# Context keys and values in one stage, and norm factors taken up by the last projection

## What is computed

```python
hc = rms_norm(h_ctx, norm_g[l]) * (1.0 + scale_c) + shift_c
...
kv = hc @ w_in[l][:, ATT_W:ATT_W + 2 * KV_W]
kc_raw, vc_raw = kv[..., :KV_W], kv[..., KV_W:]
```

```python
yb = rmsnorm(o_b.reshape(B, S, HG_WIDTH), hg_norm_w[l]) * jax.nn.silu(hg_g)
...
yc = (yc + ssd_d[l][:, None] * xs_h).reshape(B, S, SSD_WIDTH) * jax.nn.silu(ssd_z)
yc = rmsnorm(yc.reshape(B, S, SSD_GROUPS, SSD_WIDTH // SSD_GROUPS), ...)
y = jnp.concatenate([ya, yb, yc], axis=-1) @ w_out[l]
x = x + gate[:, None] * y
return rmsnorm(x, final_norm_w)
```

## Time and profile before

| | us |
|---|---|
| median of 3 runs (4582.68 to 4587.5) | 4583.03 |
| the profiled execution | 4579.17 |
| its span | 4577.5 |
| TensorE busy | 3936.8 (86%) |
| VectorE busy | 2498.4 (55%) |
| ScalarE busy | 1578.3 (34%) |
| GpSimd busy | 1141.5 (25%) |

### The profile page before, as it was taken

One profiled execution on the slowest core, in us unless ns is written; L12 is line 12 of the kernel. 1 busy time (PEld: TensorE's weight loads), 2 busy tenths in 40 slices (PEclk: granted clock), 3 DMA queues, 4 the chain that ended last, 5 costly groups with the idle time before them and its releaser, 6 DMA issues. The chain is left out here.

```text
span 4577.5 us, 51311 instructions
## 1 busy us (share of the span) xinstructions
PE 3936.8 (86%) x19136; PEld 3218.8 (70%) x19136; DVE 2498.4 (55%) x3386; ACT 1578.3 (34%) x2597; POOL 1141.5 (25%) x972
## 2 busy tenths in 40 slices
PE   4659998798795999879879699999997967776998
PEld 1548886687574888668748588878886656665886
DVE  2635943687374594368736653330000479995564
ACT  2332102676221210267622222241111755554331
POOL 0421110121111111012111111111110048885454
PEclk8879999899897999989989899999998979998999
DMA  5342122422473212242246511231121365554553
GB/s 215 123 140 74 74 79 79 105 58 71 152 244 130 73 74 79 79 105 59 65 153 215 183 69 70 82 143 69 69 78 64 129 152 148 148 138 154 183 191 113
DMA packets 315680, 529.46 MB, mean 116 GB/s; under 512 B 26806, under 2 KB 203574, under 8 KB 299512
## 3 DMA queue, kind: packets, MB, share of 16 engines
q1 hardware_dynamic: 276874, 353.84, 24.9%
q0 software_dynamic: 38592, 172.82, 10.1%
HBM read 373.57 MB, written 153.00 MB: 115 GB/s over the span
## 5 line engine op out<-in xcount | busy, mean ns | idle before, releaser
L455 PE MATMUL in_ps<-h,in_wp 128*128 128x512 f32 x6624 | 1508.2, 390 | 9.9 <-POOL in_wp L620 9.9
L455 PEld LDWEIGHTS in_ps<-h,in_wp 128*128 128x128 f32 x6624 | 1246.8, 188 | 271.2 <-POOL in_wp L620 11.6
L1696 PE MATMUL out_ps<-out_y,out_wp 128*128 128x512 f32 x2976 | 691.7, 394 | 32.1 <-ACT out_y L1551 26.9
L1696 PEld LDWEIGHTS out_ps<-out_y,out_wp 128*128 128x128 f32 x2976 | 564.2, 190 | 159.3 <-issue 32.3
L590 DVE SCALAR_TENSOR_TENSOR cy<-cu,in_cw,cy 128x2048 f32<-128x2048 f32 x120 | 314.5, 2621 | 4.3
L880 PE MATMUL att_O<-att_pT,att_vs 128*128 128x512 f32 x960 | 302.6, 424 | 0.0
L518 ACT ACTIVATE in_ob<-in_ps 128x2048 f32<-128x2048 f32 x37 | 69.7, 1885 | 664.1 <-PE in_ps L455 664.1
L1613 POOL TENSOR_TENSOR out_wp<-out_w,out_wp 128x2048 fp32r<-128x2048 f32 (+1 forms) x48 | 192.6, 4011 | 412.7 <-ACT out_wp L1544 412.6
L620 POOL TENSOR_TENSOR in_wp<-in_w,in_wp 128x1024 fp32r<-128x1024 f32 x75 | 201.7, 2691 | 291.0 <-ACT in_wp L468 255.1
L1004 DVE TENSOR_TENSOR att_pT<-att_T,att_pT 128x512 fp32r<-128x512 f32 x320 | 219.5, 686 | 74.1 <-ACT att_pT L933 65.8
L1959 DVE TENSOR_SCALAR hi_z<-hi_z 128x4 f32<-128x4 f32 x1 | 0.2, 169 | 463.2 <-ACT hi_z L1916 463.2
(11 more groups left out here) (483 smaller groups left out, 6262.7 us busy)
## 6 DMA issues: line engine op xcount, KB each, us to landing
in_w<-in_w_in SPq DMA_DIRECT2D x75, 512.0 KB, 3.5
gates<-in_ob POOLq DMA_DIRECT2D x36, 1024.0 KB, 4.2
out_w<-in_w_out SPq DMA_DIRECT2D x32, 1024.0 KB, 4.9
out_mw<-in_w_ada_rows SPq DMA_DIRECT2D x48, 512.0 KB, 3.8
att_qf<-q SPq DMA_DIRECT2D x64, 256.0 KB, 4.3
out_yr<-y SPq DMA_DIRECT2D x16, 1024.0 KB, 7.0
x<-out_x POOLq DMA_DIRECT2D x64, 256.0 KB, 3.9
out_yr<-y SPq DMA_DIRECT2D x32, 512.0 KB, 5.6
```

The source lines that it names most:

```text
L455: mm = nc.tensor.matmul(ps[:, q, c * W:(c + 1) * W], wp[:, q, i, k], h[:, j, k, c * W:(c + 1) * W], start=(n + k == 0), stop=(n == 2 and k ...
L1696: mm = nc.tensor.matmul(ps[:, u % NB, :W], wp[:, u % NW, a, k], y[:, c % 2, b, k], start=(i + k == 0), stop=(i == 2 and k == KY - 1))
```

## The change

It has two parts that don't touch each other.

The first replaces the two stages of the second layer's context by one, `context_keys` (names `ckc_`). SP loads the norm row, half of x, the weights of the keys, the other half of x, the weights of the values. ScalarE copies the weights' heads in one instruction each and between them the heads of h, GpSimd makes the weights' rests, and TensorE makes the values right behind the keys.

```diff
-            sp.dma_start(wt[:], w).then_inc(w_in, 16)
...
+            sp.dma_start(rb[:], row_d.broadcast_to([P, N])).then_inc(row_in, 16)
+            for i, w in enumerate((wk_d, wv_d)):
+                half = slice(i * KH, (i + 1) * KH)
+                sp.dma_start(x[:, half], x_d[half].rearrange("k p t -> p k t")).then_inc(x_in[i], 16)
+                sp.dma_start(wt[:, i], w).then_inc(w_in[i], 16)
...
+        @block.scalar
+        def _(act):
+            for i in range(2):
+                act.wait_ge(w_in[i], 16)
+                nc.scalar.activation(wp[:, i, 0], wt[:, i], ACT.Copy).then_inc(led, 1)
+                for k in range(i * KH, (i + 1) * KH):
+                    act.wait_ge(scaled, k + 1)
+                    nc.scalar.activation(h[:, 0, k], x[:, k], ACT.Identity, bias=shift[:, k:k + 1]).then_inc(headed, 1)
```

```diff
-            def hscale(c):
-                dve.wait_ge(hrooted, c + 1)
-                tt(ho[:, c % 2], ho[:, c % 2], bcast(hrs[:], H), mul).then_inc(hscaled, 1)
...
-            def norm(u):
-                dve.wait_ge(rooted, u + 1)
-                tt(o[:, u % 4], o[:, u % 4], bcast(rs[:], GT), mul).then_inc(normed, 1)
...
             def store(u):
                 c, g = u // 2, u % 2
-                pool.wait_ge(normed, u + 1)
+                pool.wait_ge(gated, u + 1)
...
+            def factors(u):
+                sp.wait_ge(rooted, u + 1)
+                sp.dma_start(norm_d[1 + u % 2:2 + u % 2, at(u // 2)], rs[0:1, u % 4]).then_inc(rs_out[u % 4], 16)
```

In the last projection:

```diff
             def piece(c, p):
                 m = c * G + p
+                if scaled(c, p) is not None and (p - PLAIN) % 2 == 0:
+                    r = (p - PLAIN) // 2
+                    wait(sp, yscaled, scaled(c, p))
+                    sp.dma_start(rn[:], norms[r:r + 1, cols(c)].broadcast_to([P, W])).then_inc(rn_in, 16)
                 wait(sp, yparted, m - 1)
                 sp.dma_start(yr[:, m % 2], y_d[p * KP:(p + 1) * KP, :, cols(c)].rearrange("k p t -> p k t")).then_inc(y_in[m % 2], 16)
...
-                act.wait_ge(y_in[m % 2], 16 * (m // 2 + 1))
+                if scaled(c, p) is None:
+                    act.wait_ge(y_in[m % 2], 16 * (m // 2 + 1))
+                else:
+                    act.wait_ge(yscaled, scaled(c, p) + 1)
...
-                for a in ahead(u):
-                    piece(*a)
+                catch_up = norms is not None and c and n == SQUARE_AT
+                if not catch_up:
+                    for a in ahead(u):
+                        piece(*a)
...
+            def take(c, p):
+
+                if scaled(c, p) is None:
                     return
+                m = c * G + p
+                dve.wait_ge(y_in[m % 2], 16 * (m // 2 + 1))
+                dve.wait_ge(rn_in, 16 * (c * GROUPS + (p - PLAIN) // 2 + 1))
                 for i in range(KP):
                     k = p * KP + i
-                    ins = stt(y[:, c % 2, 1, k], yr[:, m % 2, i], y_gain[:, k:k + 1], y[:, c % 2, 0, k].bitcast(F32), ALU.mult, ALU.subtract)
-                ins.then_inc(yparted, 1)
+                    ins = stt(yr[:, m % 2, i], yr[:, m % 2, i], y_gain[:, k:k + 1], rn[:], ALU.mult, ALU.mult)
+                ins.then_inc(yscaled, 1)
...
             for p in range(G):
-                piece(0, p)
+                take(0, p)
+                if norms is None:
+                    piece(0, p)
+                elif p:
+                    piece(0, p - 1)
```

More of the change, by code:

```diff
@@ L1483, in fresh, with scaled @@
             return u < U and (not kept or u < KT)
+        PLAIN = 2
+        GROUPS = (G - PLAIN) // 2
+        def scaled(c, p):
+            return c * (G - PLAIN) + p - PLAIN if norms is not None and p >= PLAIN else None
         def ahead(u):
@@ L1604, in _ @@
                         square(v)
+                if catch_up:
+                    for a in ahead(u):
+                        piece(*a)
             root(NCH - 1)
@@ L1796, in _ @@
                 for a in ahead(u):
-                    piece(*a)
+                    take(*a)
+                    if norms is None:
+                        piece(*a)
                 add(u)
+                if norms is not None:
+                    for a in ahead(u):
+                        piece(*a)
                 gather(u)
@@ L2180, in _ @@
                     hload(c + 2)
+                if unit(T - 4) is not None:
+                    factors(unit(T - 4))
+                if late(T - 2) is not None:
+                    hfactors(late(T - 2))
+            for T in range(TICKS, TICKS + 5):
+                if unit(T - 4) is not None:
+                    factors(unit(T - 4))
+                if late(T - 2) is not None:
+                    hfactors(late(T - 2))
+            for r in range(4):
+                sp.wait_ge(rs_out[r], 16 * (U // 4))
+            for r in range(2):
+                sp.wait_ge(hrs_out[r], 16 * (C // 2))
         @block.gpsimd
@@ L2569, in _ @@
                 hg(3)
-                if unit(T - 2) is not None:
-                    norm(unit(T - 2))
-                if late(T) is not None:
-                    hscale(late(T))
         @block.tensor
```

173 lines of the change are left out of this document (94 added, 79 removed).

## The result

The changed kernel takes 4590.8 us (median of 20 runs, 4583.2 to 4601.0), the kernel before, beside it, 4583.0 (20 runs, 4576.1 to 4587.5): a ratio of 1.0017, 95% interval 1.0011 to 1.0024. That is 7.9 us more, where 25 less were forecast; the range, 4541 to 4576, misses it by 15. The profiled execution took 4583.6 us (span 4582.0), 4.5 more than the one of before.

A forecast was written before the change was run, and what follows sets the result against it. VectorE was taken to bound the recurrences and TensorE the last projection. Terms -36 (recurrences), -9 (context), +17 and +3 (last projection) sum to -25: 4554 us profiled, 4558 by the median, range 4541 to 4576.

The forecast's parts named there:

- The recurrences, -36: Recurrences: 48 norm multiplications gone from VectorE save 34 us, the stage's end 2; together -36, from -20 to -41.
- the end of the stage: End of the recurrences: GpSimd's 1.90 us wait for the last norm before the last store goes; 2 us taken, bounds 0 and 3.
- rival 2: Recurrences: GpSimd or the chain product, pick, output becomes the bound; gain 12 in place of 36, time 4582; chance 0.12.
- rival 3: Last projection: scaled piece delays the weights' copy in every unit of three blocks; 45 in place of 3, 4600; chance 0.07.
- whether that time vanishes with the operation or falls on the next one: Recurrences: VectorE's standing still for GpSimd in the removed norms, left open between 27.6 and 38.2 us; 34 taken.
- Context keys and values, -9: Second layer's context stages joined: -7 with values at half clock, -11 if the clock rises early; -9, from -4 to -12.
- The start of the last projection, +17: Last projection's first pieces of y: one load in flight, period 6.6 us in place of 4.1; +17, from +11 to +22.
- The 2 us put down for the clock: Start of the last projection: TensorE, underworked between pieces, stands at half clock when it goes on; 2 us more.
- The rest of the last projection, +3: Last projection, blocks 1 and 2: weights' copy behind a scaled piece, about 2 us of waiting each; +3, from 0 to +10.
- the 1 us given back: Rest of the last projection: the norm row in PSUM takes a block's last scalings out of GpSimd's way, about 1 us back.
- The sign: Whole kernel: faster than before 0.83, within 0.1, slower 0.07.
- rival 1: Start of the last projection: the pieces are not the bound, the start costs 4, time 4545; chance 0.13.

The follow-up runs named there:

- e10: Kernel before with the joined context stage and, in the recurrences, output behind turn and exponents without VectorE's wait; norms stay on VectorE: 29.4 us under the kernel before.
- e9: Changed kernel with all that e5, e6 and e7 changed: 4534.1 us against 4579.1 for the kernel before.
- e5: Changed kernel without VectorE's wait for the output, output moved behind turn and exponents, VectorE's products of x ahead of its gates: 19.9 us under the kernel before.
- e4: Changed kernel whose first VectorE difference of a chunk no longer waits for the output of the chunk before: 11.2 us over the kernel before.
- e2: Kernel before with the norms' part alone (factors stored by the recurrences, multiplied in the last projection), old context stages: 23.7 us over the kernel before.
- e3: Changed kernel, VectorE splitting each piece of y right behind its scaling at the last projection's start: 6.4 us over the kernel before.
- e6: Changed kernel with e3's order, and the row of factors asked for behind the first load of y of its pair: 1.8 us under the kernel before.
- e8: Changed kernel as it is, timed again and profiled a second time: 9.9 us over the kernel before, recurrences 494.8 us.
- e7: Changed kernel, ScalarE copying the last projection's weights ahead of its copy of y's next piece: 2.8 us over the kernel before.
- e1: Kernel before with the joined context stage alone: 9.8 us under the kernel before.
- e11: Changed kernel with e5's order on TensorE and VectorE, but VectorE's wait for the output kept: 10.1 us under the kernel before.

## Why the prediction was wrong

**The recurrences, -36: the failed step.** The prediction prices the 46 norms that "lie where VectorE has no gaps" at VectorE's own time, 27.6 to 38.2 us. VectorE had no gaps, but 99% busy did not make its work the thing that sets the pace. The term measured -13.8 in the first profile, -5.4 in the second, and -20 with the path mended (e10 to e9 and e5). In the first profile its small part, the end of the stage, came to -3.1 for -2, so the 34 measured 10. Two things are wrong in it. First, the ring through the output was named (rival 2, "the chain product, pick, output"), given 0.12, and set aside because GpSimd and TensorE "are seen waiting for VectorE", with a fifth to spare. A ring needs no busy engine: it is made of a stretch on each, and each waits for the one before it. Rival 2's 12 us is near what the first profile shows. Its 4582 is the nearest of the times named, 9 us under the measured one; rival 3's 4600 is as near by luck, since no wait for weights in every unit was there. (The Trainium skill, "Perfetto Trace Analysis", Identifying the Most-Contended Engine, says to work first on the engine with the highest occupancy, and takes occupancy on VectorE for a fair measure. The prediction reasoned the same way, and e4, e5 and e10 show where it misleads: VectorE at 99% gave 17 us of stage to a change of order alone.) Second, "whether that time vanishes with the operation or falls on the next one": it fell on other ones (0.9 us a chunk, e5 against e10), while the value taken, 34, lay nearer the bound at which it vanishes.

**The clock in the recurrences: not in the prediction at all.** TensorE stood 2.38 us ahead of the output in the kernel before too, and kept the upper level there. With the norms gone and the output early, five of seven profiles (e2, e3, e4, e6, e8) had 5 or 6 of the 16 outputs at the lower level, 8 to 10 us in all; e7 and the first profile had none. In those five every low output but the very first of e8 stands behind 2.38 us without a product. Such stops from the fifth or sixth chunk on come before every second output, where in e7 and the first profile they come before every fourth. But the kernel before had them before every second output, too, from the sixth on, and kept the upper level, so why some executions have it and others don't stays open. e1 had it in 2 of 16 with the norms in place.

**Context keys and values, -9: right.** The stage fell by 11.2 and the kernel by 9.8 (e1). The values' products began at 1447.8 (1447.3 worked out; the prediction's own steps add up to 1447.0). They took 5.87 us. The clock rose within the first third of them, as reckoned: it was at the lower level up to about 1448.6, which makes 0.84 of full on average from 1448 to 1450, and at the upper one behind that:

```profile
1447.79 5.87 PE L720 MATMUL ckc_ps<-ckc_wp,ckc_h 128*128 128x128 f32 x48
...
1448.00:1450.00 2.00, 2.00 (x17) 2.00 (x17) 0.00 (x0) 0.38 (x1) 0.00 (x0) 0.84 0.23 70
```

That is not so in every execution. In e1, e10 and e11 the same products, behind the same keys, stayed at the lower level to their end, and the stage took 32.5 to 32.9 us, 7 less than before. In e1:

```profile
1445.80 10.34 PE L720 MATMUL ckc_ps<-ckc_wp,ckc_h 128*128 128x128 f32 x48
```

The prediction had both values, -7 and -11, and took -9 between them, so this term was right by its mechanism and rests on the clock for 4 us. The other profiles with the joined stage show 27.5 to 29.1. Why the clock rises in some isn't known.

**The start of the last projection, +17: right.** Period 6.57 (6.6), first full unit 16.3 later: 0.9 up to the third piece's scaling, 12.4 for the five pieces, 2.9 from there to the unit, where 0.6, 12.6 and 1.4 were worked out. The 2 us put down for the clock can't be seen as such. It did fall between the pieces (0.74 of full from 4193 to 4214), but the first full unit ran at the upper level, 16 products in 3.90 us. The cause, one load in flight in place of two, is shown by e3 and e6 in the period, and only in part in the unit's start: with the order mended the period is 5.28, and with the queue behind the factors mended too, 4.44. The second of these, a load standing behind the row of factors, the prediction had not seen, since the first hid it.

**The rest of the last projection, +3: mis-sized.** The mechanism, a copy of y ahead of the weights' copy at the start of blocks 1 and 2, was right and in the right place, but it cost 3.75 + 3.05 us in place of 2 + 2, and the 1 us given back did not show. Of the stage's +26.6, 16.3 is the start, 0.9 the wait behind the first unit's first products, 6.8 these waits; 2.6 is not placed.

**The sign.** Put together: -11 for the context, -14 to -5 for the recurrences, +27 for the last projection. The last of these alone was sure to eat a small gain, and the forecast's sign hung on the one term that was read from a share of busy time. Two slips in the chances change nothing of this: 4558 with the low end of the recurrences is 4574, not 4576, and half of rival 2 with the forecast and rival 1 makes 0.87 for faster, not 0.83.

## What to carry to other kernels

Before pricing work that is taken from an engine, follow one period around: who waits for whom from one chunk to the next. An engine at 99% may be filling gaps that another path leaves, and where two engines hold each other up, as VectorE and GpSimd do here, part of its busy time belongs to the other. If a disturbance of a known size (here a low clock in 16 products) lengthens the period by its full size, what it disturbs is on the path: move that first, then take work off. Of a load that is to be multiplied before it is used, look at what its buffer's release waits for and what stands ahead of it in its queue, since two loads in flight become one easily.

## What was not expected of the hardware

TensorE's granted clock fell to its lower level (1.2 GHz) at the first product behind an idle of 2.4 us, for some 3.4 us, in some executions, and stayed at the upper one behind the same idle in others (rows of e8 and of the first profile above). Behind the same stretch of products at the start of the joined context stage's values it rose in nine of twelve profiles and did not in three (5.87 and 10.34 us for the same 48 products). VectorE's subtraction of two SBUF operands of 128x256 took 733 ns on average beside GpSimd's sums and 520 without them. Removing VectorE's norms (e10 to e5) lengthened the same kind of subtraction from 692 to 734 ns.
